# A two-block network in fp32 on one core: recurrence heads, output chunks, MLP weight splits and rope keys reordered

## The reference, cut to what matters

```python
# block 1: rms norm, gated conv, gated linear recurrence, w_o, then
h = rms_norm(x, g_mlp); x = x + square(relu(h @ w_1)) @ w_2        # "mlp0"
x = rms_norm(x, g_final)
# block 2, layer 1: HGRN2, 8 heads of 128, states carried over chunks of time
q = silu(xn @ w_q); forget = lb + (1 - lb) * sigmoid(xn @ w_f)
k = 1 - forget; v = xn @ w_i; b = cumsum(log(forget))             # in a chunk
o = (q * exp(b)) @ state + (scores with decay exp(b_t - b_s)) @ v
state = exp(b_last) * state + (k * exp(b_last - b)).T @ v
h = h + (rmsnorm(o) * silu(xn @ w_g)) @ w_o                       # "hwo"
h = h + square(relu(rmsnorm(h) @ w_up)) @ w_down                  # "mlp1"
# block 2, layer 2: attention, 16 heads; k_rope is shared by all heads
s = (q_nope @ k_nope.T + q_rope @ k_rope.T) * scale               # 128 + 64 wide
h = h + (softmax(causal s) @ v) @ w_o;  h = h + mlp(h)            # "mwo", "mlp2"
```

## Time and profile before

| | |
|---|---|
| Median of 3 runs | 2478.06 us (2476.28 to 2479.21) |
| Profiled execution, its own time | 2478.5 us |
| Its span, first to last instruction | 2476.7 us |
| PE busy | 2339.2 us, 94% |
| DVE, ACT, POOL busy | 1231.2, 858.8, 864.3 us |
| Mean granted TensorE clock | 0.971 of full speed |
| HBM | 191.01 MB read, 78 GB/s over the span |

### The profile page before, as it was taken

How to read it: one execution, slowest core, us unless ns; L and a number is a source line. 1 busy time by engine, 2 the same in 40 slices (tenths; PEclk the granted TensorE clock), 3 DMA queues, 4 the chain that set the end, 5 groups by cost and what they waited for, 6 DMA issues and landing times.

```text
span 2476.7 us, 29880 instructions
## 1 busy us (share of the span) xinstructions
PE 2339.2 (94%) x10216; PEld 1840.8 (74%) x10216; DVE 1231.2 (50%) x1873; ACT 858.8 (35%) x1074; POOL 864.3 (35%) x189
## 2 busy tenths in 40 slices
PE   7999998699999999899979999999899999999998
PEld 5888776577788887778767788887566668788887
DVE  3999257625332237787755332235555531422333
ACT  4322366323221225354433221224444432222223
POOL 2343434253444433222213443434311113434342
PEclk9999999899999999899979999999999999999999
DMA  3223221132323232212112323232211103222322
GB/s 125 95 92 102 85 61 44 51 102 94 102 85 98 88 102 80 56 52 67 51 34 79 102 85 102 85 102 72 60 30 34 30 21 102 85 95 92 102 85 102
DMA packets 232934, 193.84 MB, mean 78 GB/s; under 512 B 18224, under 2 KB 228656, under 8 KB 232880
## 3 DMA queue, kind: packets, MB, share of 16 engines
q1 hardware_dynamic: 232016, 191.92, 24.6%
q10 hardware_dynamic: 864, 1.21, 0.2%
HBM read 191.01 MB, written 2.10 MB: 78 GB/s over the span
## 4 chain that ended last, share of the span: by engine, by line
issue 60%; PE 26%; POOL 13%; ACT 1%; DVE 0%; POOLq 0%; DMA 0%; DVEq 0%; SPq 0%; ACTq 0%
POOL w_lo L535 13%; PE ps L1449 6%; PE ps L1451 6%; PE ps L1450 6%; PE ps L1482 2%; PE ps L1483 2%; PE ps L1484 2%; PE ps L1514 0%; ACT w_hi L556 0%; DMA x_tm<-in_x 0%; DVE tmp L325 0%; POOLq L545 0%; PE ps L1442 0%; PE ps L314 0%; DVE y_tm L1429 0%
## 5 line engine op out<-in xcount | busy, mean ns | idle before, releaser
L535 POOL TENSOR_TENSOR w_lo<-raw,w_hi 128x2048 fp32r<-128x2048 f32 x184 | 862.3, 4687 | 1583.8 <-ACT w_hi L556 1583.8
L556 ACT ACTIVATE w_hi<-raw 128x2048 fp32r<-128x2048 f32 x184 | 351.3, 1910 | 542.4 <-PE ps L1451 298.6
L1449 PE MATMUL ps<-XH,w_hi 128*128 128x512 f32 x1128 | 449.8, 399 | 8.5 <-POOL w_lo L535 5.1
L1451 PE MATMUL ps<-XH,w_lo 128*128 128x512 f32 x1128 | 446.7, 396 | 0.0
L1450 PE MATMUL ps<-XL,w_hi 128*128 128x512 f32 x1128 | 446.5, 396 | 0.0
L1449 PEld LDWEIGHTS ps<-XH,w_hi 128*128 128x128 f32 x1128 | 212.2, 188 | 63.6 <-POOL w_lo L535 6.4
L1450 PEld LDWEIGHTS ps<-XL,w_hi 128*128 128x128 f32 x1128 | 212.3, 188 | 52.9 <-issue 1.4
L1451 PEld LDWEIGHTS ps<-XH,w_lo 128*128 128x128 f32 x1128 | 212.0, 188 | 52.1
L1137 DVE TENSOR_TENSOR X<-X,ps 128x512 f32 x72 | 49.5, 688 | 339.5 <-PE ps L1451 176.8
L1482 PE MATMUL ps<-XH,w_hi 128*128 128x512 f32 x448 | 182.5, 407 | 11.8 <-DVE XL L330 10.2
L690 ACT ACTIVATE FH<-tmp 128x512 f32 x96 | 60.7, 633 | 382.1 <-DVE tmp L1123 382.1
(11 more groups left out here) (319 smaller groups left out, 3572.4 us busy)
## 6 DMA issues: line engine op xcount, KB each, us to landing
raw<-in_mlp_w_down SPq DMA_DIRECT2D x68, 512.0 KB, 4.1
raw<-in_w SPq DMA_DIRECT2D x64, 512.0 KB, 4.1
raw<-in_mlp_w_up SPq DMA_DIRECT2D x64, 512.0 KB, 4.2
raw<-in_w_in SPq DMA_DIRECT2D x56, 512.0 KB, 4.4
raw<-in_mla_w_o SPq DMA_DIRECT2D x16, 512.0 KB, 4.6
raw<-in_w_b_out SPq DMA_DIRECT2D x16, 384.0 KB, 4.0
raw<-in_w_a_out SPq DMA_DIRECT2D x8, 512.0 KB, 4.4
raw<-in_w_o SPq DMA_DIRECT2D x8, 512.0 KB, 3.9
```

Source lines behind the costliest of these rows:

```text
L535: pool.tensor_tensor(w_lo[:, s], raw[:, s], w_hi[:, s].bitcast(F32), ALU.subtract)\
L556: act.activation(w_hi[:, s], raw[:, s], ACT.Copy).then_inc(hi_done, 1)
L1449: pe.matmul(dst, his[k], xh[k], start=start and k == 0, stop=False)
L1451: mm = pe.matmul(dst, los[k], xh[k], start=False, stop=stop and k == n - 1)
```

## The change

1. Heads: `turn_values(h)` moves from the end of head h-1 to behind the gate projection of h+1, and the copy of the values on ACT (`values_act`) from behind the square to the head's start. `rest_pe(h+1)` is cut in two, the states of h between the halves; DVE chains them (`states_dve`) in the middle of `decays_dve(h+1)`.
2. Last head: in place of a next head's projections, PE computes hwo's first two chunks in pieces; hwo's remaining two follow.
3. Start: the split of chunk `hg`+2 moves ahead of the norm's Ln; `turn_values(0)` goes into head 0. A new tile `FR` keeps the norm's inverse root, so that DVE scales one tile of `X` in each head instead of eight before the loop.
4. MLPs: the split of chunk 2 moves ahead of the inverse root (`sum_act`), and out of the first part of the loop.
5. Rope keys: `KR` keeps the upper 64 partitions zero, `KR_ODD` the lower ones; all rope products contract over 128 rows.

```diff
+        KR_ODD, _ = place("KR_ODD", [P, T], F32, a_rst + TILE)
...
             def sum_act(st, chunks, n, gain, off=0, xh=XH):
+                m = n[2:]
...
                     square_act(act, n, k)
+                split_hi(FIRST[m] + 2, 0)
                 rest_act(act, n)
...
+                def part(q, i, first=False):
+                    for j in range(4):
+                        act.wait_ge(*at(n, "t", 8 * q + 4 * i + j + 5))
+                        act.activation(FH[:, bass.ds(4 * i + j, 1)], tmp[:, j % 2:j % 2 + 1], ACT.Square)\
+                            .then_inc(sig(n, "fh"), 1)
+                        if j % 2 and not (first and j == 1):
+                            split_hi(8 * q + 2 * i + c + j // 2 + 2, j // 2)
...
+            split_hi(FIRST["hg"] + 2, 0)
             act.preload_act_table_set(LN_EXP)
...
-                act.activation(rst[:, n], rst[:, n], ACT.Exp, scale=-0.5).then_inc(s_("f_r"), 1)
+                act.activation(FR[:] if n == 0 else rst[:, 1], rst[:, n], ACT.Exp, scale=-0.5).then_inc(s_("f_r"), 1)
...
             def head_act(h, n, more=True):
+                values_act(h, n)
                 if more:
                     gates_act(h + 1)
...
                 act.activation(tmp[:, 0], ps[:, 6], ACT.Square).then_inc(s_("h_sq"), 1)
-                if more:
-                    values_act(h + 1, 1 - n)
...
                     .then_inc(s_("h_kd_arg"), 1)
+                if between is not None:
+                    between()
                 for l, m in enumerate(LEVELS):
...
                 if more:
-                    decays_dve(h + 1, 1 - n)
+                    decays_dve(h + 1, 1 - n, lambda: states_dve(h, n))
                     rest_dve(h + 1, 1 - n)
...
                     decayed_dve(h + 1, 1 - n)
+                else:
+                    states_dve(h, n)
+                dve.scalar_tensor_tensor(X[:, bass.ds(h, 1)], X[:, bass.ds(h, 1)], dcol("g_final", h),
+                                         FR[:].rearrange("p (a t) -> p a t", a=1), ALU.mult, ALU.mult)
...
-            for k in range(KD):
-                dve.scalar_tensor_tensor(X[:, k], X[:, k], col("g_final", k), rst[:, 0], ALU.mult, ALU.mult)\
-                    .then_inc(chain.sem, 1)
...
+            kc.put(dve.memset(KR_ODD[0:ROPE], 0.0))
+            kc.put(dve.tensor_copy(KR_ODD[ROPE:P], KR[ROPE:P]))
+            kc.wait()
+            kc.put(dve.memset(KR[ROPE:P], 0.0))
             kc.wait()
             small_norm_dve("ckv", CK, "kv_norm_2", CKH, CKL)
...
+            def first_out(ks):
+
+                chunk_in(c_o)
+                pair(0, 0, OH, OL, lambda k: (s_("ho_done"), k + 1), ks)
...
             def head_pe(h, n, more=True):
+                pe.wait_ge(s_("h_q0"), h + 1)
+                pe.wait_ge(s_("h_f0"), h + 1)
                 if more:
-                    pe.wait_ge(s_("h_q0"), h + 1)
-                    pe.wait_ge(s_("h_f0"), h + 1)
                     gates_pe(h + 1)
+                else:
+                    first_out(range(7))
+                turn_values(h)
...
+                pe.wait_ge(s_("h_g0"), h + 1)
+                pe.wait_ge(s_("h_v"), h + 1)
                 if more:
-                    pe.wait_ge(s_("h_g0"), h + 1)
-                    pe.wait_ge(s_("h_v"), h + 1)
-                    rest_pe(h + 1)
+                    rest_pe(h + 1, range(4))
+                else:
+                    second_out(range(2))
                 pe.wait_ge(s_("h_kt_c"), h + 1)
-                pe.wait_ge(s_("h_v"), h + 1)
                 for b in range(3):
                     mm = pe.matmul(ps[:, 7, b * P:(b + 1) * P], HKT[:, b], HV[:, n, b], start=True, stop=True)
                 mm.then_inc(s_("h_st"), 1)
+                if more:
+                    rest_pe(h + 1, range(4, KD))
+                else:
+                    second_out(range(2, 3))
...
                 mm.then_inc(s_("h_o"), 1)
-                if more:
-                    turn_values(h + 1)
+                if not more:
+                    second_out(range(3, 4))
                 pe.wait_ge(s_("h_sq"), h + 1)
                 pe.matmul(ps[:, 7], ones[:], tmp[:, 0], start=True, stop=True).then_inc(s_("h_mean"), 1)
+                if not more:
+                    second_out(range(4, 7))
+                    first_out(range(7, KD))
+                    second_out(range(7, KD))
...
-                    r = slice(ROPE * (h % 2), ROPE * (h % 2) + ROPE)
+                    kr = (KR, KR_ODD)[h % 2]
...
-                        pe.matmul(ps[:, b, 0:n], QR[r, h // 2, b * P:n], KR[r, 0:n], start=False, stop=True)\
+                        pe.matmul(ps[:, b, 0:n], QR[:, h // 2, b * P:n], kr[:, 0:n], start=False, stop=True)\
                             .then_inc(att("a_qk", 0)[0], 1)
```

More of the change, by code:

```diff
@@ L684, in mlp_act, with down @@
                 c = FIRST[n]
[L686 to L696, removed]
+                def part(q, i, first=False):
[5 more added lines that the diff above has]
+                            split_hi(8 * q + 2 * i + c + j // 2 + 2, j // 2)
+                def down(q):
                     with act.Fori(0, 2) as i:
@@ L699, in mlp_act @@
                             split_hi(8 * q + 2 * i + c + 6 + s, s)
-                up(3)
+                part(0, 0, first=True)
+                part(0, 1)
+                down(0)
+                with act.Fori(1, 3) as q:
+                    with act.Fori(0, 2) as i:
+                        part(q, i)
+                    down(q)
+                with act.Fori(0, 2) as i:
+                    part(3, i)
                 for k in range(KD):
@@ L741, in gates_act @@
                 act.activation(HF[:], HF[:], ACT.Sigmoid).then_inc(s_("hf_sg"), 1)
-                split_hi(2 * h + c + 2, 0)
+                if split:
+                    split_hi(2 * h + c + 2, 0)
             def out_gate_act(h, n):
@@ L1225, in levels_dve, with states_dve, decays_dve @@
                             ps[:, 4 + (l - 1) % 2, 0:256].rearrange("p (g t) -> p g t", t=m)).then_inc(s_("h_g_free"), 1)
-            def decays_dve(h, n):
+            def states_dve(h, n):
+                dve.wait_ge(s_("h_st"), h + 1)
+                for b_ in range(3):
+                    st = ps[:, 7, b_ * P:(b_ + 1) * P]
+                    if b_ == 0:
+                        dve.tensor_copy(HS[:, 0], st).then_inc(s_("h_s"), 1)
+                    else:
+                        dve.wait_ge(s_("h_s"), 3 * h + b_)
+                        dve.scalar_tensor_tensor(HS[:, b_], HS[:, b_ - 1], HEB[:, n, b_ * P + P - 1:b_ * P + P], st,
+                                                 ALU.mult, ALU.add).then_inc(s_("h_s"), 1)
+            def decays_dve(h, n, between=None):
                 dve.wait_ge(s_("hq_sg"), h + 1)
@@ L1471, in half8, with pair @@
                 product(ps[:, bank], w8(w_hi, s, n), w8(w_lo, s, n), tiles(xh), tiles(xl)).then_inc(halves, 1)
-            def pair(s, bank, xh, xl, ready=None):
+            def pair(s, bank, xh, xl, ready=None, ks=range(KD)):
                 h = [w8(w_hi, s, n) for n in range(2)]
                 l = [w8(w_lo, s, n) for n in range(2)]
-                for k in range(KD):
+                for k in ks:
                     if ready is not None:
@@ L1615, in gates_pe, with rest_pe, second_out @@
                 pair(0, 0, XH, XL, lambda k: at("n_hg", "lo", k + 1))
-            def rest_pe(h):
+            def rest_pe(h, ks=range(KD)):
                 chunk_in(2 * h + c + 1)
-                pair(1, 2, XH, XL)
+                pair(1, 2, XH, XL, ks=ks)
+            c_o = FIRST["hwo"]
+            def first_out(ks):
+                chunk_in(c_o)
+                pair(0, 0, OH, OL, lambda k: (s_("ho_done"), k + 1), ks)
+            def second_out(ks):
+                chunk_in(c_o + 1)
+                pair(1, 2, OH, OL, lambda k: (s_("ho_done"), k + 1), ks)
             def turn_values(h):
@@ L1684, in _ @@
             rest_pe(0)
-            turn_values(0)
             with pe.Fori(0, HEADS_H // 2 - 1) as i:
@@ L1690, in _ @@
             head_pe(7, 1, more=False)
-            plain(FIRST["hwo"], 2, lambda v: at("hwo", "x", v), OH, OL, lambda k: (s_("ho_done"), k + 1))
+            for j in range(2):
+                chunk_in(c_o + 2 + j)
+                pe.wait_ge(*at("hwo", "x", 4 + 2 * j + 2))
+                half8(j, 0, 2 * j, OH, OL)
+                half8(j, 1, 2 * j + 1, OH, OL)
             mlp_pe("mlp1", XH, XL)
```

27 lines of the change are left out of this document (9 added, 18 removed).

## The result

The changed kernel takes **2452.45 us** (median of 4 runs, 2444.89 to 2452.96) against 2478.64 for the kernel before in the same session (4 runs): **ratio 0.9897, 95% interval 0.9883 to 0.9912**. Timed once more in another session it had 2448.90 (ratio 0.9880, 0.9864 to 0.9897). Forecast: 2451.6 in a range of 2434 to 2465.

The account below looks back on a forecast made before the run. PE, busy 94% of the span, was taken as the bound, so its waits were counted: 2478.5 + 1.5 (repeated heads) - 9.8 (head 0) - 10.8 (last head) - 6.8 (MLPs) - 2.3 (attention) + 1.3 (ahead of it) = 2451.6 us; range 2434 to 2465.

Parts of the forecast that it names:

- +0.2 a head: Repeated heads: period 36.2 instead of 35.99, taken as 0.2 more for each of 7 heads, +1.5 us.
- queue chain: Repeated heads: table load and states delay ACT's sigmoid, exponentials and split, so the square starts at G + 23.4.
- lower bound of 34.9 for a hidden table load: Repeated heads: period 34.9, 7.6 us less in all, if the table load stays hidden.
- 6.0 named as the possible gain: Head 0: another 6.0 us beyond the 9.8 taken, if the wait of 2.9 does not lower the clock.
- The 4.3 put there: Last head: clock cost behind the wait of 2.6 ahead of short matmuls, between nothing and 8.6, taken as 4.3 us.
- the loop: Attention: a head's period is a 9.3 us loop through DVE and ACT; padding shortens it by only 0.3 a head.
- feared loss behind the first head's wait of 2.73: Attention: each iteration's first head waits 3 instead of 0.8 for a POOL-blocked division, perhaps lowering the clock; 1.3 us back.
- Table load hidden: Rival: everything at full clock with the table load hidden, 2431 us; chance 0.17 together with a free softmax.
- Slower by the attention's clock: Rival: PE's idle of 1.2 per attention head brings 1.2 GHz throughout, 87 us in 16 heads, 2539; chance 0.05.
- softmax does not bind: Rival, attention: padding brings 1.3 to 1.5 a head, 27 us instead of 2.3, 2427; chance 0.17 together with full clock.
- padding brings nothing: Rival, attention: 32-row weight loads take as long as 128-row ones, so no gain, 2455; chance within the forecast's 0.55.
- the splits do not come earlier: Rival, MLPs: splits stay late behind ACT's own waits, the 6.8 us stay, 2458; chance 0.19 together with low-and-longer heads.

Follow-up runs that it names:

- table: Changed kernel with the sigmoid's table set loaded ahead of the copy of the values instead of behind it; 2437.04 us, ratio 0.9856 to the kernel before.
- u_hg: Changed kernel without the early split of head 0's gate weights; 2446.22 us, ratio 0.9882 to the kernel before.
- al: Changed kernel with the attention's low part of the head before subtracted between two row maxima instead of behind the divisions; 2442.56 us, ratio 0.9840 to the kernel before.
- u_pad: Changed kernel with the rope padding undone (64-row products, no KR_ODD); 2456.57 us, ratio 0.9932 to the kernel before.
- u_fill: Changed kernel without pieces of hwo in the last head, all four chunks running behind it; 2468.48 us, ratio 0.9967 to the kernel before.
- table_split: Changed kernel with the table load ahead of the values' copy and ACT's split of slot 1 behind the square; 2433.75 us, ratio 0.9814 to the kernel before.
- late: Changed kernel with the chained states behind the levels' arguments, still in mid-projection; 2441.79 us, ratio 0.9844 to the kernel before.
- split: Changed kernel with ACT's split of slot 1 moved behind the square, table load left in place; 2450.75 us, ratio 0.9912 to the kernel before.

## Why the prediction came out right

**Repeated heads: wrong in size.** The step that failed is "+0.2 a head", a sum without a term for the clock. The queue chain was right to 0.1, and 36.15 was seen where the clock stayed up. But the new wait is 2.54, in one piece, where before 1.68 and 0.25 stood apart, and it costs 1.5 to 1.6 of clock nearly every time; the period is 37.7, 1.7 more than before. The prediction had applied the same worry to head 0 and the last head ("every idle of 2 us or more in a stretch like these was followed by a low one") and did not turn it on the wait that its own sum made 2.1 long (24.05 less 21.95; the outputs end at 21.5, so it is 2.54). Its upper bound of 37.0 was passed, and so was its own sign of being wrong, a period over 36.6. Missed: 6.8. Its lower bound of 34.9 for a hidden table load does not follow from its terms either: 21.95, 0.65 and 12.15 make 34.75, and the states in front of the arguments still push by 0.96. `table` measured 35.25.

**Head 0: right, clock on the better side.** 7.7 of 7.7 for the start; the wait of 2.14 went as forecast. The low stretch behind the wait of 2.99 lasted 3.4 us in the profiled run: 5.2 more of the 6.0 named as the possible gain. In nine of the twelve kernels run, with this same wait, it lasted 13.7 to 17.1, and the next scores came 41.8 to 43.4 behind instead of 36.98. That difference, 4.8 to 6.4, is near the 7 between the changed kernel's 2445 to 2446 and its 2452. The longer executions do differ by the clock: a mean granted clock of 0.974 over a span of 2450.3 is 63.7 us lost, 0.977 over 2443.1 is 56.2, and the 7.5 between them is about all of the difference. That it is lost in the levels of head 0 is argued, not shown, as these executions have no trace. If it is, the low levels that the forecast took were the common case, and the profiled execution the lucky one.

**Last head and hwo.** Ahead of the clock the forecast was 18.0, and 17.9 was measured to the third chunk; its waits of 1.52 and 5.25 were forecast as 1.35 and 5.2. In part the agreement is luck: the first wait is 0.81 instead of 2.6, and the low stretch behind the mean of head 6, for which the sum has no term, takes about as much. Where that stretch does not come (`u_hg`, `al`, `u_pad`) the first wait is 2.42 to 2.44. The clock cost 1.8 behind the 5.25 (2.9 forecast) and nothing in the levels. The 4.3 put there is mis-sized, and not because the wait was short: in every run that keeps the filling the levels of the last head take 6.4 to 6.7, also behind waits of 2.4 to 3.4. Without the filling and behind 7.26 they take 12.05 (`u_fill`).

**MLPs, attention, front.** 7.6 for 6.8 forecast; 4.9 for 2.3, of which the loop gave 0.36 a head (0.3 forecast) and the feared loss behind the first head's wait of 2.73 did not come as a sum: low stretches of 6.8 lie in two of the four iterations instead of three. Where they fall differs between executions, and in the other traces with this attention the stage takes 254.1 to 257.8 (256.5 here). Ahead of the attention two memsets and the copy take 1.6 (1.3 forecast).

**The rivals.** "Table load hidden" named what could still be won, but hiding the load alone gives 35.25 (`table`); 34.65 a head takes the later split as well (`table_split`). "Slower by the attention's clock" fell: idles of 1.18 in eight heads were followed by no low stretch. That softmax does not bind fell with `al`, where a shorter loop shortens the head by 0.6. That padding brings nothing fell with `u_pad`, and that the splits do not come earlier with the three waits that are gone.

## What to carry to other kernels

Price a new wait twice, once as idle and once as what it does to PE's clock behind it, and do it above all for waits that your own sum creates. When a step moves to the head of a queue, everything that rode in the shadow of the old wait (here a table load of 1.28) must find a new shadow; one preload call gave back 2.45 a head, where the reordering of the heads could have given 1.1 by the prediction's own bound. After removing a wait, compute the round of each engine by itself: with ACT's chain up to the square the period is 36.15 at full clock, with DVE's 35.28, with PE's 34.6, and fixing one alone can lose to the next.

## What the runs showed of the hardware

- One idle of 2.5 to 2.6 ahead of the mean was followed by 3.4 us at 1.2 GHz in 37 of 40 repeated heads (heads 1 to 5 in eight traces of seven kernels); one of 1.63 never was in `table`, nor 1.16 and 0.69 apart in `late`. Waits of 0.78 and 0.74 within short level matmuls were, in `split`, and one of 0.70 there was not.
- The length of the idle alone does not say it. The same wait of 3.37 ahead of hwo's seventh tile had a low stretch of 6.8 us in `split` and none in `table_split` (a row of PE and the clock from there on, first in `split`, then in `table_split`):

```profile
1258.80 0.79 PE L1504 MATMUL ps<-OH,w_hi 128*128 128x512 f32 x1 [3.37 <-DVE OL L1326]
1258.80:1264.80 6.00, 6.00 (x22) 5.31 (x23) 0.37 (x1) 2.16 (x3) 0.00 (x0) 0.50 0.21 72
...
1246.97 0.50 PE L1505 MATMUL ps<-OH,w_hi 128*128 128x512 f32 x1 [3.37 <-DVE OL L1327]
1247.00:1257.00 10.00, 10.00 (x80) 9.58 (x81) 4.30 (x9) 2.07 (x4) 0.00 (x0) 1.00 0.12 40
```

- The same wait of 2.99 ahead of the same matmuls had a low stretch of 3.4 us in three profiled executions (the changed kernel in two sessions, `table`) and of 13.7 to 17.1 in nine.
- Without padding a weight load over 64 rows stood 0.76 on "issue" behind products over 128 rows, and its product of 512 columns took 1.05; padded to 128 rows it takes 0.86.
